# A two-block transformer kernel: one turning of a token tile for two norms, and a wait split by pairs of chunks

## The reference

```python
def shared_kv(h, norm_g, w_kvf, ...):        # first block, layer 1
    s = rms_norm(h, norm_g)                  # norm "KV"
    kvf = s @ w_kvf                          # k, v, forget gates
def mixer_b(x, k, v, ..., w_in, ...):
    qg = x @ w_in                            # x = rms_norm(h, b_norm_g), norm "B", of the SAME h
def hybrid_layer(x, mem, pos, g_mix, w_in, ...):   # second block, run twice
    h = rms_norm_2(x, g_mix)
    z = h @ w_in                             # norm "X"
```

## Time and profile before

| | us |
|---|---|
| median of 3 runs (lowest, highest) | 2361.95 (2361.78, 2362.13) |
| profiled execution, its own time | 2362.53 |
| its span, first to last instruction | 2360.7 |
| PE busy | 2346.1 (99%) |
| DVE busy | 1699.0 (72%) |
| ACT busy | 1413.8 (60%) |
| mean granted TensorE clock | 0.999 |

### The profile page before, as it was taken

How to read it: one execution, slowest core, us unless ns; L and a number is a source line. 1 busy time by engine, 2 the same in 40 slices (tenths; PEclk the granted TensorE clock), 3 DMA queues, 4 the chain that set the end, 5 groups by cost and what they waited for, 6 DMA issues and landing times.

```text
span 2360.7 us, 28287 instructions
## 1 busy us (share of the span) xinstructions
PE 2346.1 (99%) x11214; PEld 1953.9 (83%) x11214; DVE 1699.0 (72%) x1497; ACT 1413.8 (60%) x1372; POOL 36.0 (2%) x23
## 2 busy tenths in 40 slices
PE   9999999999999999999999999999999999999998
PEld 7788888888788888888888888878888888888887
DVE  6655555856999898989898999976466556547554
ACT  5544444665777777777777777765645445564542
POOL 1000000001000000000000000000010000001000
PEclk9999999999999999999999999999999999999999
DMA  8455555434999999999999999945345554534552
GB/s 292 151 185 174 196 193 179 161 124 178 351 370 358 357 365 373 366 351 365 371 368 346 370 366 370 368 182 194 110 158 176 184 190 181 180 107 170 196 178 107
DMA packets 82034, 587.85 MB, mean 249 GB/s; under 512 B 9280, under 2 KB 9424, under 8 KB 11376
## 3 DMA queue, kind: packets, MB, share of 16 engines
q1 hardware_dynamic: 81040, 582.11, 66.5%
q0 software_dynamic: 864, 3.93, 0.5%
HBM read 584.94 MB, written 1.05 MB: 248 GB/s over the span
## 4 chain that ended last, share of the span: by engine, by line
PE 95%; DVE 3%; ACT 1%; issue 0%; DMA 0%; SPq 0%; DVEq 0%; ACTq 0%
PE U L1783 15%; PE U L1785 15%; PE U L1784 15%; PE Y L1783 14%; PE Y L1785 14%; PE Y L1784 14%; PE T L2070 1%; PE Y L2040 1%; PE T L1960 1%; PE T L2334 1%; DVE w_lo L1100 1%; PE T L1949 1%; PE U L2056 1%; PE Y L2043 1%; ACT w_hi L706 0%
## 5 line engine op out<-in xcount | busy, mean ns | idle before, releaser
L1100 DVE TENSOR_TENSOR w_lo<-raw,w_hi 128x2048 fp32r<-128x2048 f32 x211 | 482.2, 2289 | 221.8 <-ACT w_hi L706 221.8
L706 ACT ACTIVATE w_hi<-raw 128x2048 fp32r<-128x2048 f32 x214 | 410.1, 1922 | 223.5 <-PE Y L1785 108.5
L1783 PE MATMUL U<-w_hi,x_hi 128*128 128x512 f32 x1312 | 514.8, 392 | 1.8 <-DVE x_lo L1152 0.7
L1785 PE MATMUL U<-w_lo,x_hi 128*128 128x512 f32 x1312 | 510.9, 389 | 0.0
L1784 PE MATMUL U<-w_hi,x_lo 128*128 128x512 f32 x1312 | 510.7, 389 | 0.0
L1546 DVE TENSOR_TENSOR w_lo<-arena,w_hi 128x2048 fp32r<-128x2048 f32 x192 | 437.9, 2291 | 51.3 <-ACT w_hi L955 51.1
L955 ACT ACTIVATE w_hi<-arena 128x2048 fp32r<-128x2048 f32 x192 | 368.2, 1918 | 111.1 <-PE U L1785 69.5
L1783 PE MATMUL Y<-w_hi,t_hi 128*128 128x512 f32 x1000 | 396.7, 397 | 0.5 <-DVE w_lo L1546 0.5
L1785 PE MATMUL Y<-w_lo,t_hi 128*128 128x512 f32 x1000 | 390.4, 390 | 0.0
L1784 PE MATMUL Y<-w_hi,t_lo 128*128 128x512 f32 x1000 | 389.5, 389 | 0.0
L1546 DVE TENSOR_TENSOR w_lo<-raw,w_hi 128x2048 fp32r<-128x2048 f32 x144 | 329.1, 2291 | 39.9 <-ACT w_hi L955 39.7
(11 more groups left out here) (281 smaller groups left out, 2155.7 us busy)
## 6 DMA issues: line engine op xcount, KB each, us to landing
arena<-in_w_expert SPq DMA_DIRECT2D x192, 1024.0 KB, 5.6
raw<-in_w_expert SPq DMA_DIRECT2D x144, 1024.0 KB, 5.7
raw<-in_w_layer SPq DMA_DIRECT2D x126, 1024.0 KB, 4.8
raw<-in_w_first SPq DMA_DIRECT2D x88, 1024.0 KB, 4.9
arena<-in_mem SPq DMA_DIRECT2D x2, 1024.0 KB, 4.9
arena<-in_gv POOLq DMA_DIRECT2D x1, 1536.0 KB, 10.0
h<-in_x SPq DMA_DIRECT2D x2, 512.0 KB, 5.8
raw<-in_w_first SPq DMA_DIRECT2D x2, 512.0 KB, 5.8
```

Source lines behind the costliest of these rows:

```text
L706: act.activation(w_hi[:, s, :], raw[:, s, :], ACT.Copy).then_inc(hi_ready, 1)
L1100: dve.tensor_tensor(w_lo[:, s, :], raw[:, s, :], w_hi[:, s, :].bitcast(F32), ALU.subtract).then_inc(lo_ready, 1)
L1783: pe.matmul(acc, a_hi, b_hi, start=first, stop=False)
L1785: return pe.matmul(acc, a_hi, b_lo, start=False, stop=last)
```

## The change

`nB` 2 and 3 are no longer turned. They are named as the next contents of the banks that hold `nKV` 2 and 3, and are split a second time from there with the gain of norm B, into `t_hi` and `t_lo`. Their place in all three orders moves ahead of `nB` 0 and 1. In `up_moved`, for `nX` alone, PE waits first for two of a group's four chunks and for the other two in the middle of the unit.

```diff
-           + [("nKV", g) for g in range(4)] + [("nB", g) for g in range(4)] + [("fT", 0)]
+           + [("nKV", g) for g in range(4)] + [("nB", g) for g in (2, 3, 0, 1)] + [("fT", 0)]
...
             root("KV", NT)                                     # ACT
+            split_rows("nB", t_hi, gains(G_B), start=2)
...
             evac_part(QKVG[0], pair(0))
             split_rows("nB", t_hi, gains(G_B), groups=2)
             ahead(("kv", 1, 0))
-            split_rows("nB", t_hi, gains(G_B), start=2)
...
                             last = dve.scalar_tensor_tensor(lo_d[:, k0 + i, tok], ...   # DVE, split_rows
+                            if name == "nX" and i == 1:
+                                last.then_inc(x_half, 1)
...
+            split_rows("nB", t_hi, t_lo, gains(G_B), start=2)  # DVE
             ahead(("kv", 0, 1))
             split_rows("nB", t_hi, t_lo, gains(G_B), groups=2)
             ahead(("kv", 1, 0))
-            split_rows("nB", t_hi, t_lo, gains(G_B), start=2)
             ahead(("kv", 1, 1))
...
                     pe.wait_ge(lo_ready, used((*key, hf), l))  # PE, up_moved
-                    pe.wait_ge(t_done, filled((name, 2 * t + hf), l))
-                    last = up_tile(key, hf, t, banks, x_hi, x_lo)
+                    if name == "nX":
+                        pe.wait_ge(x_half, 4 * l + 2 * t + hf + 1)
+                        rest = filled((name, 2 * t + hf), l)
+                    else:
+                        pe.wait_ge(t_done, filled((name, 2 * t + hf), l))
+                        rest = None
+                    last = up_tile(key, hf, t, banks, x_hi, x_lo, rest=rest)
...
                 for q in range(4):                             # PE, up_tile
+                    if rest is not None and q == 2:
+                        pe.wait_ge(t_done, rest)
...
-                    last.then_inc(t_filled, 1)                 # PE, turn_rows
+                    last.then_inc(t_filled, 3 if (name, g) == ("nKV", 3) else 1)
...
                     if n == 2:
-                        pe.wait_ge(t_done, filled(("nB", 3)))
+                        pe.wait_ge(t_done, filled(("nB", 1)))
                         forget_rows()
...
                         up_unit(QKVG[n], hf, pair(n), ...)
-                        if n == 1 and hf == 0:
-                            turn_rows("nB", h, start=2)
```

More of the change, by code:

```diff
@@ L463, in program @@
         bo_half = sem("bo_half")
+        x_half = sem("x_half")
         out_half = sem("out_half")
@@ L1812, in h_tile, with up_tile @@
                 return lambda t: pe.wait_ge(h_done, h_no(stage, t, l))
-            def up_tile(key, hf, t, banks, a_hi, a_lo, in_halves=False):
+            def up_tile(key, hf, t, banks, a_hi, a_lo, in_halves=False, rest=None):
                 s = unit_slot(UNITS[(*key, hf)])
```

## The result

| | before | changed |
|---|---|---|
| median of 22 runs, us | 2361.85 | 2365.62 |
| lowest, highest | 2361.37, 2362.45 | 2364.11, 2366.84 |
| profiled execution, own time | 2362.53 | 2365.59 |
| its span | 2360.7 | 2363.8 |

The ratio is 1.0016 (95% interval 1.001 to 1.0022): slower by 3.8 us, within the 0.2% that counts as no change here, inside the range 2362.8 to 2367.0, and 1.0 us above the forecast of 2364.6. The changed kernel's executions are spread over 2.7 us where those of before are spread over 1.1, and they lie in groups: 4 of 22 at 2364.1 to 2364.5, 16 at 2365.3 to 2366.2, 2 at 2366.7 and 2366.8. The first group is where the forecast lies, 2.4 above before. The medians hide this. The profiled execution is of the second group; no trace of the changed kernel is of the first.

What follows compares the result with a forecast made beforehand. The prediction took PE, busy 99% of the span, as the bound. Its terms -0.98 + 3.60 + 0 + 0 = +2.62 us on the median 2361.95 gave 2364.6, with a range of 2362.8 to 2367.0.

Steps and rivals of the forecast that it cites:

- Part 1: Between units (kv,1,0) and (kv,1,1): eight transposes of nB 2 and 3 go, with their wait; -0.98 us.
- Part 2: Before nB 0 and 1 are turned: PE waits for DVE's second split of nB 2 and 3; +3.60 us.
- Part 3: Work behind the new splits on ACT and DVE: moves later but stays covered, 3 us spare for (kv,1,1); 0.
- Part 4: Norm X, first layer: x by pairs gains nothing, as w_lo's wait grows from 0.59 to about 1.1; 0.
- The bound of -0.55: Norm X, first layer: all of the 0.65 wait for x but its latency kept to the end; rival chance 0.05.
- The clock: In the new gap at nB: 2.8 us of unbroken idle time, so the granted clock should hold; no cost.
- that rival: The clock falls in the new gap at nB: 2.62 + 2.0 = +4.6, 2366.6 us; chance 0.12.
- The rule named there: For the gap at nB: no idle gap of this length between bursts of products; following it gives 2366.6 us.
- The hidden-wait rival: At nB: the new wait is hidden and only the removed turning counts, -0.98, 2361.0 us; chance 0.10.

Runs made afterwards that it cites:

- e6: The changed kernel with nB 2 and 3 split ahead of the row factors on ACT and DVE; 2360.94 us, -0.9 against before.
- e5: The changed kernel with eight transposes of h put back between the two units of (kv,1); 2366.31 us, +4.5 against before.
- e3: The changed kernel without its second part, PE waiting for all four chunks of x as before; 2365.44 us, +3.6 against before.
- e4: The kernel before with only the second part, x of norm X awaited by pairs of chunks; 2361.98 us, ratio 1.0001.
- e7: As e6, with the first layer's rest of the second (in,0) unit made and awaited in two halves; 2360.08 us, -1.7 against before.
- e8: The kernel before with only that weight rest made and awaited by halves, x awaited whole; 2361.45 us, -0.35 against before.
- e10: The changed kernel with DVE making the rest of (kv,1,1) ahead of the second splits; 2370.95 us, +8.95 against before.
- e9: As e7, with the first layer's unit (in,1,1) rounded by ACT ahead of its root; 2359.84 us, -2.2 against before.
- e1: The changed kernel with twelve useless matmuls in PE's new wait before nB 0 is turned; 2364.33 us, +2.5 against before.
- e2: The changed kernel with four useless matmuls in PE's new wait before nB 0 is turned; 2365.00 us, +3.2 against before.

## Why the prediction was right, and where it was not

- **Part 1, the turning:** forecast -0.98; -1.14 by e6's stretch; put back in e5 it costs 0.95. Right.
- **Part 2, the new wait:** forecast +3.60; 428.38 - 423.84 - 1.00 = +3.54 in the changed kernel, +3.50 in e3, +3.51 against e6. Both releases came when forecast. Right, with some luck in one step: the 1.20 from ACT's start to DVE's was read where DVE was busy with w_lo until 429.91, so it was not a latency there; the changed kernel, where DVE does wait for ACT, has 1.17. With part 1 it gives the 2.4 of the lowest group (forecast 2.62), as e3's trace with its full clock does (15.29 - 12.92 = 2.37).
- **Part 3, what moves behind:** no further wait of PE up to the forget rows in any of the traces; the changed kernel's products from 432.6 to 440.8 stand 0.23 apart. Right.
- **Part 4, pairs of x:** forecast 0 with the wait moved to w_lo, 1.1; e4 shows both. Right. The bound of -0.55 is about what the pairs are worth once the rest is made by halves: 0.67 - 0.17 = 0.50 by the stretches of e7 and e8. Only 1.07 - 0.89 = 0.18 of it is an earlier start of tile (0,1); the other part is a shorter wait for (in,1,1), which the forecast did not have.
- **The clock: wrong.** The prediction named a fall of the clock at nB as a sign of being wrong, and the clock fell there. The result still lies in the range because the range was drawn to take in that rival, not because the forecast's account was whole: 2365.62 lies just above the 2363.8 to 2365.5 that it gave to the forecast itself. The step that failed is "here the unbroken idle time is 2.8, so the clock should hold". It took one fall, 3.6 us behind the last product at the end of the span, for a limit. The traces have three more: near 427.9 in e10, 2.9 us behind its last product (424.66 + 0.39); near 428.5 in e5, 4.0 us behind its last (424.07 + 0.39; the clock column is 0.74 over 428 to 429); and near 428.9 in the changed kernel, 4.7 us behind its last (423.84 + 0.39) and half a microsecond after products had begun again. So one fall is no limit, the delay is not fixed, and the turning of eight chunks in between did not save it. The rival had the price nearly right, 2.0 for 1.6, in part by luck: it was read from the first nine products of the kernel, over which the clock column shows 1.00, so those rows don't price a lowered clock. It should have had most of the chance instead of 0.12: 18 of 22 executions lie above 2365.3. The sum of the sizes, -1.1 + 3.5 + 1.6 = +4.0, is the +4.04 by which the changed kernel's stretch exceeds that of before. The rule named there, from the Trainium skill (TensorE: Matmul & The Clock Gate, section "Why this matters for your kernels"), which warns of a gap of this length, was the better guide. The changed kernel's trace agrees with it (3.17 us idle, and a fall); e3's does not (3.12 us idle, and the full clock).
- **The hidden-wait rival** (2361.0) did not happen in the change and is what e6 does (2360.94). Its condition, the first new split on ACT before 421.5, is met there (418.36).

What stays open: why two executions of the changed kernel and three of e3 lie at 2366.7 to 2367.0, more than one fall of 1.6 explains. Their mean clocks are 0.997 to 0.998; none of them was the profiled one.

## What to carry to other kernels

Before a step is dropped because its data already lies in a bank, ask who must now release that bank, and where that work stands in the releaser's order. Here 1 us of transposes was traded for 3.5 us of waiting, because the second reading was queued behind a root that waits for a reduction; moved ahead of it, the same change gains. A gap of 2.3 to 3.2 us on a PE that is otherwise busy had a second price here, some 1.6 us of half-rate products, that came in some executions and not in others; look at the groups among the runs, not only at the median, and at the clock in more than one trace. When an awaited thing is made earlier, look at what is awaited next: here pairs of x needed the weight rest by halves (e7), and that one needed a unit ahead of root (e9).

## What the runs showed of the hardware that was not expected

The granted clock can fall after products have resumed (428.9, with products from 428.4), so a gap's damage may begin behind the gap. With 2.7 of 3.2 idle microseconds filled by useless products none of 11 executions is slower by the price of a fall (e1, spread 0.7 us); with 0.9 filled about half are (e2).
